# A decoder step on one core: pooling unit by unit, three map banks, first loads a stage ahead, fixed addresses, inverse with interleaved updates

## What is computed

```
sol = lax.linalg.triangular_solve(lower, rhs, left_side=True, lower=True, unit_diagonal=True)
...
for gi, w in enumerate(POOL_WINDOWS):           # windows 2, 4, 8, 16; 384 channels each
    lo, hi = gi * POOL_GROUP, (gi + 1) * POOL_GROUP
    start = csum[:, POOL_BUF + 1 - w:POOL_BUF + 1 - w + T, lo:hi]
    count = jnp.minimum(float(w), pos + 1.0)[None, :, None]
    diffs.append((end[..., lo:hi] - start) / count - uf[..., lo:hi])
d = jnp.stack(diffs, axis=2)
y = jnp.einsum('btgc,gce->btge', d, w_pool.astype(jnp.float32)).reshape(B, T, POOL_WIDTH)
return (y * pool_scale.astype(jnp.float32)).astype(u.dtype), ext[:, ext.shape[1] - POOL_BUF:]
...
merged = (gates[:, :, 0] * (o_a @ wb[:DN_WIDTH])
          + gates[:, :, 1] * (o_b @ wb[DN_WIDTH:DN_WIDTH + SWA_OUT])
          + gates[:, :, 2] * (o_c @ wb[DN_WIDTH + SWA_OUT:]))
x = x + merged @ w_out[l]
```

## Time and profile before

| | us |
|---|---|
| three runs: lowest, median, highest | 5772.64, 5780.05, 5784.27 |
| profiled execution, its time | 5772.16 |
| its span | 5770.4 |
| PE busy in the span | 4837.8 (84%) |
| DVE, ACT, POOL busy | 2981.2, 1248.2, 1530.5 |

### The profile page before, as it was taken

One profiled execution on the slowest core, in us unless ns is written; L12 is line 12 of the kernel. 1 busy time (PEld: TensorE's weight loads), 2 busy tenths in 40 slices (PEclk: granted clock), 3 DMA queues, 4 the chain that ended last, 5 costly groups with the idle time before them and its releaser, 6 DMA issues. The chain is left out here.

```text
span 5770.4 us, 50751 instructions
## 1 busy us (share of the span) xinstructions
PE 4837.8 (84%) x17538; PEld 2851.2 (49%) x17538; DVE 2981.2 (52%) x7204; ACT 1248.2 (22%) x3129; POOL 1530.5 (27%) x1406
## 2 busy tenths in 40 slices
PE   7889998898997787777787899988989877777776
PEld 5776676665542333322166757766655422322221
DVE  4532211213669999755454222112146799996554
ACT  2211220102222333211112112201022233332111
POOL 0221100001444444434303111000024444444432
PEclk9889998999999999999999899989999999999999
DMA  2212242315999999999812122323169999999997
GB/s 95 74 54 65 69 128 72 98 58 195 395 392 420 420 420 418 415 420 420 347 61 74 53 74 69 125 70 109 43 249 388 403 420 420 420 419 414 420 420 306
DMA packets 338619, 1432.13 MB, mean 248 GB/s; under 512 B 27389, under 2 KB 156279, under 8 KB 190443
## 3 DMA queue, kind: packets, MB, share of 16 engines
q0 software_dynamic: 177376, 1268.07, 54.1%
q1 hardware_dynamic: 155054, 157.63, 8.6%
q10 hardware_dynamic: 5932, 3.19, 0.2%
HBM read 1400.16 MB, written 49.44 MB: 251 GB/s over the span
## 5 line engine op out<-in xcount | busy, mean ns | idle before, releaser
L2184 PE MATMUL ps<-early,diag 128*128 128x512 f32 (+1 forms) x3328 | 1571.7, 619 | 390.4 <-ACT diag L2115 390.1
L2035 POOL DMA_INDIRECT early<-in_peer,ids x832 | 913.6, 1098 | 2124.7 <-PE ps L2184 1171.8
L2184 PEld LDWEIGHTS ps<-early,diag 128*128 128x128 f32 (+1 forms) x3328 | 607.8, 190 | 1310.8 <-issue 662.7
L2059 DVE SCALAR_TENSOR_TENSOR early<-early,rows 128x1024 f32<-128x1024 f32 x832 | 1004.8, 1223 | 382.7 <-DMA early<-in_peer,ids 381.6
L2184 PE MATMUL ps<-late,diag 128*128 128x512 f32 (+1 forms) x1280 | 610.5, 622 | 185.0 <-ACT diag L2115 184.8
L2115 ACT ACTIVATE diag<-consts_sb,weight 128x128 f32<-128x128 f32 (+1 forms) x1152 | 392.5, 388 | 651.9 <-DVE weight L2069 638.6
L2184 PEld LDWEIGHTS ps<-late,diag 128*128 128x128 f32 (+1 forms) x1280 | 228.5, 188 | 564.9 <-ACT diag L2115 311.5
L2059 DVE SCALAR_TENSOR_TENSOR late<-late,rows 128x1024 f32<-128x1024 f32 x320 | 386.8, 1223 | 160.3 <-DMA late<-in_peer,ids 159.9
L2035 POOL DMA_INDIRECT late<-in_peer,ids x320 | 344.2, 1075 | 455.9 <-PE ps L2184 432.3
L1157 PE MATMUL ps<-hT,gate_ring 128*128 128x288 f32 x1536 | 410.0, 422 | 0.0
L2107 ACT ACTIVATE gel<-dot 128x2 f32<-128x2 f32 x576 | 117.3, 204 | 1261.5 <-DVE early L2059 859.1
(11 more groups left out here) (349 smaller groups left out, 5481.8 us busy)
## 6 DMA issues: line engine op xcount, KB each, us to landing
ring<-in_w_in SPq DMA_DIRECT2D x14, 2048.0 KB, 10.2
gate_ring<-in_w_in POOLq DMA_DIRECT2D x48, 512.0 KB, 4.7
ring<-in_w_in SPq DMA_DIRECT2D x12, 1536.0 KB, 6.6
ring<-in_w_branch SPq DMA_DIRECT2D x16, 1152.0 KB, 6.9
late<-in_peer_query SPq DMA_DIRECT2D x32, 512.0 KB, 7.1
gate_rows<-gate_out POOLq DMA_DIRECT2D x48, 288.0 KB, 2.4
gate<-gate_rows SPq DMA_DIRECT2D x16, 864.0 KB, 8.4
early<-in_peer,ids POOLq DMA_INDIRECT x832, 21.2
```

The lines of the kernel that those rows point to most:

```text
L2035: pool.indirect_dma_start(place(q), None, table_rows, bass.IndirectOffsetOnAxis(ap=ids[:, n, c:c + 1], axis=0)).then_inc(s.pair[PLACE[q]], 16)
L2059: nc.vector.scalar_tensor_tensor(out=up, in0=up, scalar=1.0, in1=rows[:, n, :], op0=ALU.mult, op1=ALU.mult, accum_out=dot[:, i % 2, k:k + ...
L2184: ins = nc.tensor.matmul(g.ps[0:r, 2 * (n % 2) + m, :], diag[:, q % DIAGS, 0:r], place(q)[:, D + m * 512:D + (m + 1) * 512], start=False, ...
```

## The change

The inverse takes the tiles of a step in descending order, so the youngest comes first. Between two mixes stands the update of the unit before; the unit with j = 0 is updated behind the first mix. `update` signals `inv` and `invT` apart (`inv_sum`, `pe_b`), DVE signals `inv_done` after the first subtraction, and a bank waits only for its own.

Pooling goes unit by unit, windows in the order 16, 8, 4, 2: DVE computes the sums of each unit right after its copies, GpSimd copies the tails, PE transposes them one projection later, and a group's maps stand behind the second projection of the next group, as two halves of 288 columns in three banks in turn. The first slab is loaded at the end of `window_samples`, the first three slots of the merge inside pooling, `w_out` first in the merge. All SBUF tensors get set addresses (`Room`), so that the slots of three stages share places.

```diff
+AT_MIX, AT_LATE, AT_WORK = 0, 8192, 16384
+AT_OC = AT_WORK + 16384
...
+    def __init__(self, nc, at, end):
...
+    def __call__(self, name, shape, dt=F32):
+        at = self.at
...
+        return self.nc.alloc_sbuf_tensor_at(fresh(name), shape, dt, offset=at)
...
-    steps = [[(n, k - 1 - n) for n in range(TILES) if 0 <= k - 1 - n < depth[n]] for k in range(TILES + LEVELS)]
+    steps = [[(n, k - 1 - n) for n in reversed(range(TILES)) if 0 <= k - 1 - n < depth[n]] for k in range(TILES + LEVELS)]
...
+    firsts = [unit for unit in units if unit[1] < LEVELS - 1]
+    first_part = lambda unit: firsts.index(unit) + 1
...
-                pe.wait_ge(s.dve_a, made((n, j - 1)))
+                pe.wait_ge(s.inv_done, first_part((n, j - 1)))
...
-                r, used = ROWS[n], before((n, j), units)
-                if used:
-                    pe.wait_ge(s.dve_a, used)
+                r = ROWS[n]
                 if j == 0:
                     pe.wait_ge(s.masked, made((n, j)))
-                    for h in range(H):
-                        last = nc.tensor.matmul(g.ps[0:r, inv_bank((n, j)), h * r:(h + 1) * r], heads_of(lowm, n)[:, h], ident(g, r),
-                                                start=True, stop=True)
                 else:
                     pe.wait_ge(s.act_a, mixed((n, j)))
                     pe.wait_ge(s.started, n + 1)
+                    if j > 1:
+                        pe.wait_ge(s.dve_a, mixed((n, j - 1)))
+                if j < LEVELS - 1:
+                    if before((n, j), firsts):
+                        pe.wait_ge(s.inv_done, before((n, j), firsts))
                     for h in range(H):
-                        if j < LEVELS - 1:
-                            nc.tensor.matmul(g.ps[0:r, inv_bank((n, j)), h * r:(h + 1) * r], heads_of(invT, n)[:, h], heads_of(mid, n)[:, h],
...
+                        if j == 0:
+                                                    start=True, stop=True)
...
+                    last.then_inc(s.inv_sum, 1)
+                if j > 0:
+                    if before((n, j), mids):
+                        pe.wait_ge(s.dve_a, before((n, j), mids))
+                    for h in range(H):
-                last.then_inc(s.pe_b, 1)
+                    last.then_inc(s.pe_b, 1)
...
-                for n, j in step:
-                    if j:
-                        mix(n, j)
-                for n, j in step:
-                    update(n, j)
+                ready = [unit for unit in step if unit[1] == 0]
+                for unit in [unit for unit in step if unit[1]]:
+                    mix(*unit)
+                    if ready:
+                        update(*ready.pop(0))
+                    ready.append(unit)
+                for unit in ready:
+                    update(*unit)
...
-                dve.wait_ge(s.pe_b, made((n, j)))
+                if j < LEVELS - 1:
+                    dve.wait_ge(s.inv_sum, first_part((n, j)))
+                    if j > 0:
+                        dve.wait_ge(s.inv_done, first_part((n, j - 1)))
+                    nc.vector.tensor_tensor(heads_of(inv, n), bc(ident(g, r), 1, H) if j == 0 else heads_of(inv, n),
+                                            bank(inv_bank((n, j)), r, r), ALU.subtract).then_inc(s.inv_done, 1)
+                if j > 0:
+                    dve.wait_ge(s.pe_b, mixed((n, j)))
...
-                        pool.wait_ge(s.pe_b, made((n, 0)))
+                        pool.wait_ge(s.inv_sum, first_part((n, 0)))
...
+            sp.dma_start(pool_slab(slots, 0), pool_weights(t, l, 0)).then_inc(s.pool_slab, 16)
...
+POOL_ORDER = list(reversed(range(POOL_UNITS)))
...
+    c = C_U + (POOL_SLABS - 1 - i) * 512
+    return rows_of(layer(t["w_in"], l))[:, :, c:c + 512]
...
-        ring, wp = sb("ring", [P, 2, 4096]), sb("wp", [P, 2, 3, PG])
-        ext, sums, spare = sb("ext", [P, 2, 3, UW]), sb("sums", [P, 3, UW]), sb("spare", [P, 3, UW])
...
+    sb, high = g.space(AT_WORK), g.space(AT_OC + PW // P * TOK)
+    wp, ext = sb("wp", [P, 2, 3, PG]), sb("ext", [P, 2, 3, UW])
+    sums, spare = sb("sums", [P, 2, UW]), sb("spare", [P, 2, UW])
+    diff = sb("diff", [P, 2, 3, TOK])
+    tail = sb("tail", [P, 2, 3, PBUF + NS])
+    new, old = high("new", [PBUF + NS, PW]), high("old", [NB * PBUF, PW])
...
+    group = lambda k: G - 1 - k
+    unit = lambda p: divmod(POOL_ORDER[p], 3)
+    bank_a = lambda p: g.ps[:, p % 2, 0:HALF]
+    bank_b = lambda p: g.ps[:, 2 + p % 2, 0:HALF]
+    map_bank = lambda m: g.ps[:, 4 + m % 3, 0:HALF]
...
+        @block.sync
+        def _(sp):
+            sp.dma_start(old[:], layer(t["state_pool"], l).rearrange("b j c -> (b j) c")).then_inc(s.loaded, 16)
+            sp.dma_start(pool_slab(slots, 1), pool_weights(t, l, 1)).then_inc(s.slab0, 16)
+            for k in range(2):
+                sp.dma_start(wp[:, k], rows_of(layer(t["w_pool"], l)[group(k)])).then_inc(maps_in[k], 16)
+            sp.dma_start(pool_s[:, 0:PBUF - NT], layer(t["state_pool"], l)[:, NT:PBUF]).then_inc(s.stored, 16)
+            sp.wait_ge(s.slab_free, 1)
+            sp.dma_start(pool_slab(slots, 2), pool_weights(t, l, 2)).then_inc(s.slab1, 16)
+            sp.wait_ge(s.pe_d, 6)
+            sp.dma_start(wp[:, 0], rows_of(layer(t["w_pool"], l)[group(2)])).then_inc(maps_in[0], 16)
+            sp.wait_ge(s.slab_free, 2)
+            merge.load(sp, 0)
+            sp.wait_ge(s.pe_d, 12)
+            sp.dma_start(wp[:, 1], rows_of(layer(t["w_pool"], l)[group(3)])).then_inc(maps_in[1], 16)
+            sp.wait_ge(s.slab_free, 3)
+            merge.load(sp, 1)
+            merge.load(sp, 2)
+            sp.wait_ge(s.act_c, G)
+            sp.dma_start(pool_p[0], new[0:PBUF]).then_inc(s.stored, 16)
+            for b in range(NB):
+                sp.dma_start(pool_s[b, PBUF - NT:], new[PBUF + b * NT:PBUF + (b + 1) * NT]).then_inc(s.stored, 16)
+            sp.wait_ge(s.stored, 16 * (2 + NB))
+        @block.gpsimd
+        def _(pool):
+            for k in range(G):
+                i = k % 2
+                pool.wait_ge(s.dve_a, 6 * k + 6)
+                if k >= 2:
+                    pool.wait_ge(s.pe_c, k - 1)
+                nc.gpsimd.tensor_copy(tail[:, i, :, 0:PBUF], ext[:, i, :, UP - PBUF:UP]).then_inc(s.pool_a, 1)
+                nc.gpsimd.tensor_copy(tail[:, i, :, PBUF:].rearrange("p c (b j) -> p c b j", b=NB),
+                                      ext[:, i, :, UP:UW].rearrange("p c (b j) -> p c b j", b=NB)[:, :, :, PBUF:]).then_inc(s.pool_a, 1)
...
+            def tails(k):
+                pe.wait_ge(s.pool_a, 2 * k + 2)
+                pe.wait_ge(s.dve_b, min(k + 2, G))
+                for c in range(3):
+                    last = nc.tensor.transpose(g.ps[0:PBUF + NS, 7, c * P:(c + 1) * P], tail[:, k % 2, c, :], ident(g))
+                last.then_inc(s.pe_c, 1)
+            def maps(k):
+                pe.wait_ge(maps_in[k % 2], 16 * (k // 2 + 1))
+                pe.wait_ge(s.dve_c, 3 * k + 3)
+                for c in range(3):
+                    for a in range(2):
+                        m = 6 * k + 2 * c + a
+                        if m >= 3:
+                            pe.wait_ge(s.act_d, m - 2)
+                        for i in range(3):
+                            last = nc.tensor.matmul(map_bank(m), wp[:, k % 2, i, c * P:(c + 1) * P],
+                                                    diff[:, k % 2, i, a * HALF:(a + 1) * HALF], start=i == 0, stop=i == 2)
+                        last.then_inc(s.pe_d, 1)
+                w = pool_slab(slots, p // 4)
+                if p == 0:
+                    pe.wait_ge(s.pool_slab, 16 * (l + 1))
+                elif p % 4 == 0:
+                    pe.wait_ge((s.slab1, s.slab0)[p // 4 % 2], 16)
+                if p >= 2:
+                    pe.wait_ge(s.act_a, p - 1)
+                    pe.wait_ge(s.dve_a, 2 * (p - 1))
+                for k in range(KT):
+                    weights = w[:, k, (u % 4) * P:(u % 4 + 1) * P]
+                    nc.tensor.matmul(bank_a(p), weights, g.hT[:, k, 0:HALF], start=k == 0, stop=k == KT - 1)
...
+                last.then_inc(s.pe_a, 1)
+                if p % 4 == 3:
+                    pe.wait_ge(s.pe_a, p + 1)
+                    pe.sem_inc(s.slab_free, 1)
...
+            for k in range(G):
+                raw(3 * k)
+                if k == 0:
+                    old_rows(0)
+                else:
+                    tails(k - 1)
+                raw(3 * k + 1)
+                if k:
+                    maps(k - 1)
+                raw(3 * k + 2)
+                if k + 1 < G:
+                    old_rows(k + 1)
+            tails(G - 1)
+            maps(G - 1)
...
+            for k in range(G):
+                raw(3 * k)
+                if k:
+                    rows(k - 1)
+                raw(3 * k + 1)
+                if k:
+                    scale(k - 1)
+                raw(3 * k + 2)
+            rows(G - 1)
+            scale(G - 1)
...
```

(38 more changed lines are left out.)

404 lines of the change are left out of this document (179 added, 225 removed).

## The result

| | us |
|---|---|
| after: lowest, median, highest of four runs | 5630.61, 5632.62, 5640.35 |
| before, four runs: median | 5776.35 |
| ratio, 95% interval | 0.9753 (0.9736 to 0.9770) |
| profiled execution of after: time, span | 5640.35, 5638.3 |

The change is worth 143 us, 2.5% (133 to 152 us by the interval). The forecast was 5664 with a range of 5636 to 5690: right in sign, too small by 31 us, and outside its range. The profiled executions are 132.1 us apart in span (5770.4 to 5638.3); the other 11 us are spread, since the profiled run of before is 4 us under its median and the one of after is the slowest of its four.

A forecast was written before the change was run, and what follows sets the result against it. Gathers of expert rows set the pace for some 2600 us, untouched; elsewhere PE ends last and its waits were counted. Terms sum to 111.0 us: 5661 from the profiled 5772.2, 5669 from the median; forecast 5664, range 5636 to 5690.

The forecast's parts named there:

- narrower maps: Pooling: map steps as 288 + 288 columns take 0.97 us instead of 1.08 as 512 + 64; gain 7.9 us.
- the clock: Pooling: part of the work lost at PE's lower clock level returns; gain 5 us, bounds 0 and 13.
- Start of pooling: Pooling's start: PE's waits for `old` and the first slab of `w_in` go, except the stage barrier; gain 24.1 us.
- tails: Pooling: PE's waits for DVE to copy tails and ACT to empty their bank go; gain 16.1 us.
- map bank: Pooling: nine waits a layer for ACT to empty the one output bank go with three banks; gain 17.9 us.
- merge start: Merge's start: PE's wait for `ring` goes because slots 0 to 2 are already loaded; gain 13.8 us.
- End of pooling: Pooling's end: last maps wait for the last unit's means, -5.4 us; stores behind merge loads delay the barrier, -6.4 us.
- Inverse, 38.0: Inverse: bank and `mid` waits filled by other products, less a new stall of 5.6; net 38.0 us, bounds 13 and 52.
- Rival 1: Closing gaps keeps PE's clock high in inverse step 4 and pooling: 14 + 6 us more, 5644; chance 0.13.
- Step 5: Inverse: sign to look for, this step taking 11 to 12 us where it took 20.8.
- Addresses: All SBUF buffers: same loads and sizes at other places change nothing; put at 0.
- Rival 5: Expert stages: gathers into moved buffers run slower; at 5.5% less, 150 us more, 5814; chance 0.02.

The follow-up runs named there:

- x6: The kernel after with the stores of the pooling state ahead of the loads of merge slots 1 and 2; 5633.7 us.
- x4: The kernel before with four unread products of 128 columns ahead of each update in steps 2 to 5 of the inverse; 5764.8 us, ratio 0.9985.
- x10: The kernel after with all mixes of an inverse step ahead of its updates again, tiles still descending and signals apart; median 5650.6 us.
- x1: The kernel before with the new inverse (changed `delta_chunks`) alone; 5723.8 us, ratio 0.9920.
- x2: The kernel after with the old inverse (old `delta_chunks`); 5674.5 us, ratio 0.9840.
- x5: The kernel after with the first pooling slab's load back at pooling's start; 5653.0 us, ratio 0.9792.

## Why the prediction was wrong, point by point

The step that failed is the one that turned closed gaps into time. The sum gives back PE's waits, and of PE's busy time only 7.9 us for narrower maps and 5 for the clock, both in pooling; for the inverse it has nothing. Measured, PE's busy time fell by 22.4 us in pooling and 19.4 in the inverse, 41.8 in place of 12.9. The waits came out well in pooling and too high by 9 in the inverse.

- **Start of pooling, tails, map bank, merge start (24.1 + 16.1 + 17.9, 13.8): right as waits.** PE's idle time in pooling fell from 63.8 us (356.3 less 292.5 busy) to 16.4 (286.5 less 270.1), that is 47.4, where the waits less both end terms made 46.3. The merge gave 14.1. No run takes the tails on GpSimd, the order of the windows or the early merge slots apart; these gains are read from the waits that are gone.
- **Busy time in pooling: narrower maps 7.9 and clock 5 make 12.9; it fell by 22.4.** Two things were missing. By the intervals from start to start of the matmuls, the maps gave 8 as forecast; the stops of PE, 16 fewer a layer (21 to 5), gave 4 by their drains; and the clock 8, as it rose from 0.93 to 0.96 and 0.98 (2 are not assigned). So two terms failed: the clock, put at 5 "since a wait is added at the end", and the drains, for which there was none.
- **End of pooling (-5.4, -6.4): right in size.** The first was a wait for GpSimd's tail copy (1.9 us a layer) and a short one behind it, not one wait for DVE. The second came as forecast, and the trace agrees with the rule that the prediction cites for it; another order of SP's queue does not save it (x6).
- **Inverse, 38.0: too small by 10 in the profiles and by 5 on average, with two errors of opposite sign.** PE's idle time fell by 29.0 (56.8 to 27.8 by the windows), 9 less than forecast: the wait for DVE's first part is 15.2 where the prediction has 5.6, because I worked it out for step 3 alone, and step 2 has the longest (4.4). Against it PE's busy time fell by 19.4, which was put at 0: by the intervals from start to start about 13 for the time at the lower clock level, 5 for drains, 1 not assigned. This is the term that missed most. Part of the 13 is the execution: over the 12 stretches of either list the busy time of both layers fell by 14, the clock's part being 7 to 8 of it, as the old list's clock was 0.94 on average and 0.90 and 0.92 in this profile. Rival 1 had the clock, with 14 us for the inverse, at a chance of 0.13; it was set against because the short products of the 64-row tile stay. They stay in x4 and in the new inverse too, and the clock is 0.97 to 0.99 there, so they do not hold it down. Step 5 took 12.0 us (11 to 12 forecast, 20.8 before), without a wait over 0.2:

```profile
261.76 1.06 PE L658 MATMUL ps<-inv,lowm 128*128 128x128 f32 x8
...
273.79 1.76 PE L658 MATMUL ps<-inv,lowm 64*64 64x64 f32 x16
```

- **Why the bank waits went: half right.** The interleaving was named for all of them. By x10 it is worth the 9.2 us for `mid`; the others stay away without it, by the split signals or by the descending order.
- **Addresses, 0: wrong by 9 us.** Rival 5 asked whether the rate could fall and never whether it could rise.
- **Stages not touched, 0: wrong by -10.3 in this profile and -5.6 on average.** `window_samples` has the same list on PE and the same waits, and runs at a lower clock more often in the kernels with the new inverse. Why is not settled; x1, x2 and x5 with two stretches each do not decide it.
- **The base.** I summed from the profiled execution (5772.2) and added 3; the medians say 5776 to 5780, so this did not cause the miss.

Together: busy time of the inverse +19, its waits -9, pooling +11, addresses +9, `window_samples` -10, the rest +1 make the 21 us between 132.1 and 111. Of the 31 us between 5664 and 5632.6 the other 10 are the 3 added to the base and the 8 by which the profiled execution of the kernel after lies over its median. That execution, 5640.4, is inside the range; the four runs' median is not.

## What to carry to other kernels

Where PE waits often and shortly, count three costs for each wait: its idle time, the drain before it that the view counts as busy (0.17 us here), and the granted clock of the stretch, which rose from 0.94 to 0.97 on average when the waits of the inverse went. Look at that clock over several executions, since one profile can sit at either end of its spread (0.90 to 0.99 here). Before interleaving a queue's order, try whether signals for the two halves of a pair suffice: in x10 they and the descending order kept 27.9 us of waits away without it. And look at the start address of every buffer that a long stream of transfers fills: 32 bytes of padding moved the kernel before by 42 us (ratio) to 47 (medians).

## What the runs showed of the hardware

- Transfers of 8 KB rows into buffers that start on a multiple of 256 bytes run at 427 GB/s, into buffers that start 64, 96 or 128 bytes past one at 421, 224 bytes past one at 420.
- A DVE operation with two SBUF inputs took 6.73 us instead of 0.42 beside five GpSimd operations in a row, which all went first; a copy of 128x4 took 1.26 instead of 0.17 beside one.
- With the same matmuls, PE's granted clock in the inverse was 0.90 to 0.99 (0.94 on average over 12 stretches) with 28.7 us of idle time in waits of up to 3.2 us, 0.95 to 0.98 (0.97 on average) with 13.8, and 0.99 in both layers of x4, which has products that nobody reads in them.
- A stage with an unchanged list on PE took 132.0 to 142.0 us, with a clock of 0.90 at the one end and 0.84 at the other, from run to run and layer to layer.
